# Decay and rate products of the RWKV-7 pairs issued in another order, and the key digits split later

## The reference, cut to what matters

```python
r = heads(xr @ w_rkv[0]); k = heads(xk @ w_rkv[1]); v = heads(xv @ w_rkv[2])
kk = l2_normalize(k * k_k)
for d in range(2):                       # the two directions
    logw = -softplus(-heads(w0[d] + tanh(xw @ w1[d]) @ w2[d])) - 0.5      # decay
    a = sigmoid(heads(a0[d] + (xa @ a1[d]) @ a2[d]))                      # rate
    kd = k * (1.0 + (a - 1.0) * k_a)
    dirs.append((exp(-exp(logw)), kd, -kk, kk * a))
# then, by direction: S <- S diag(w) + (S a) b^T + v k^T ; y = S r
```

## Time and profile before

| | |
|---|---|
| median of 3 runs | 2361.92 us |
| the profiled execution's own time | 2360.81 us |
| span of the profile | 2359.0 us |
| mean granted clock of PE | 0.991 |
| busy: PE, DVE, ACT, POOL | 97%, 66%, 54%, 9% |
| the RWKV-7 pairs | about 849 to 1320 us of the span |
| one pair | about 59 us |

### The profile page before, as it was taken

One profiled execution on the slowest core, in us unless ns is written; L12 is line 12 of the kernel. 1 busy time (PEld: TensorE's weight loads), 2 busy tenths in 40 slices (PEclk: granted clock), 3 DMA queues, 4 the chain that ended last, 5 costly groups with the idle time before them and its releaser, 6 DMA issues.

```text
span 2359.0 us, 57897 instructions
## 1 busy us (share of the span) xinstructions
PE 2285.1 (97%) x25130; PEld 1898.5 (80%) x25130; DVE 1561.0 (66%) x1768; ACT 1271.2 (54%) x1407; POOL 217.8 (9%) x208
## 2 busy tenths in 40 slices
PE   8999999999999889999998899999999999999998
PEld 5677566888888478888888788888888888888886
DVE  2544785322332766556666278888888888888888
ACT  4322024322222655555554277878777878777874
POOL 2000551000000041111112020000000000000010
PEclk9999999999999999999999999999999999999999
DMA  8466225333322521111102489999999999999994
GB/s 290 183 219 246 71 80 171 89 89 97 99 89 93 166 63 60 60 60 60 51 24 65 173 323 368 373 374 370 374 367 381 361 374 370 380 360 384 357 392 172
DMA packets 228493, 512.00 MB, mean 217 GB/s; under 512 B 15271, under 2 KB 108223, under 8 KB 228031
## 3 DMA queue, kind: packets, MB, share of 16 engines
q1 hardware_dynamic: 225470, 498.61, 58.3%
q10 hardware_dynamic: 1730, 7.10, 0.9%
q0 software_dynamic: 1152, 4.19, 0.6%
HBM read 492.58 MB, written 17.30 MB: 216 GB/s over the span
## 4 chain that ended last, share of the span: by engine, by line
PE 93%; DVE 3%; issue 1%; ACT 1%; DMA 1%; POOL 0%; ACTq 0%; DVEq 0%
PE bank L1700 27%; PE bank L1730 13%; PE bank L1205 3%; PE bank L1206 3%; PE bank L1207 3%; PE bank L1332 2%; PE bank L1111 2%; PE bank L1364 2%; PE bank L1082 2%; PE bank L1083 2%; PE bank L1084 2%; PE bank L1375 2%; PE bank L1223 2%; PE bank L1222 2%; PE bank L1224 2%
## 5 line engine op out<-in xcount | busy, mean ns | idle before, releaser
L3100 DVE TENSOR_TENSOR w_low<-expert_w,w_high 128x1792 fp32r<-128x1792 f32 (+2 forms) x384 | 771.8, 2024 | 121.4 <-ACT w_high L2250 118.5
L2250 ACT CAST w_high<-expert_w 128x1792 fp32r<-128x1792 f32 (+2 forms) x384 | 652.1, 1701 | 217.2 <-PE bank L1700 144.7
L1700 PE MATMUL bank<-w_high,xg_high 128*128 128x448 f32 x1024 | 294.3, 369 | 4.2 <-DVE xg_low L3090 4.2
L1700 PE MATMUL bank<-w_low,xg_high 128*128 128x448 f32 x1024 | 293.2, 368 | 0.0
L1700 PE MATMUL bank<-w_high,xg_low 128*128 128x448 f32 x1024 | 293.1, 367 | 0.0
L1700 PEld LDWEIGHTS bank<-w_high,xg_high 128*128 128x128 f32 x1024 | 191.6, 189 | 21.6 <-DVE xg_low L3090 4.4
L1700 PEld LDWEIGHTS bank<-w_high,xg_low 128*128 128x128 f32 x1024 | 192.8, 188 | 16.9
L1700 PEld LDWEIGHTS bank<-w_low,xg_high 128*128 128x128 f32 x1024 | 193.1, 189 | 15.8
L1730 PE MATMUL bank<-w_high,hid_high 128*128 128x512 f32 x448 | 175.8, 392 | 0.0
L1730 PE MATMUL bank<-w_high,hid_low 128*128 128x512 f32 x448 | 174.9, 390 | 0.0
L1730 PE MATMUL bank<-w_low,hid_high 128*128 128x512 f32 x448 | 174.7, 390 | 0.0
(11 more groups left out here) (440 smaller groups left out, 4109.3 us busy)
## 6 DMA issues: line engine op xcount, KB each, us to landing
expert_w<-in_moe_w_dram SPq DMA_DIRECT2D x128, 1792.0 KB, 9.6
expert_w<-in_moe_w_dram SPq DMA_DIRECT2D x32, 2048.0 KB, 10.3
arena<-in_mod_w_dram SPq DMA_DIRECT2D x48, 1024.0 KB, 8.6
expert_w<-in_moe_w_dram SPq DMA_DIRECT2D x32, 1536.0 KB, 10.0
arena<-in_ffn_w_dram SPq DMA_DIRECT2D x44, 512.0 KB, 5.1
slot_rows<-arena SPq DMA_DIRECT2D x25, 512.0 KB, 5.5
arena<-in_hy_w_in_dram SPq DMA_DIRECT2D x12, 1024.0 KB, 5.3
arena<-in_rw_w_rkv_dram SPq DMA_DIRECT2D x48, 256.0 KB, 2.8
```

The costliest lines, as they stand in the source:

```text
L1700: last = pe.matmul(bank[b0 + v][:, 0:EH], x[:, k, :], w_[:, kk, v * EH:v * EH + EH], start=(k == 0 and x is XGH and w_ is wh), stop=(k == ...
L2250: act.copy(high_piece(kind, n), piece(kind, ering[q % ERN], n // 2, n % 2))\
L3100: dve.tensor_tensor(piece(kind, low[s], n // 2, n % 2), piece(kind, ering[s], n // 2, n % 2), high_piece(kind, n).bitcast(F32), ALU.subtract)\
```

## The change

Four things are changed.

1. PE: `ahead_decay_and_rate` is replaced by `ahead_rate` and `ahead_decay`. The order is now decay 0, rate 0, rate 1, six fills, decay 1, each with its two column halves one behind the other. The rate of direction d goes to bank 6+d. The wait for `z_copy_0` is gone, and both rates wait for `z_copy_1`. The number of fills goes from 3 to 6, and two `settle` instructions go.
2. ACT takes the results in the order rate 0, rate 1, decay 0, decay 1.
3. POOL: the casts no longer stand before `ahead(0)` but behind the two small fills, directly before the subtractions.
4. PE: in pair 0 the wait tile by tile becomes one wait for all sixteen digit operations, ahead of the first keys product.

```diff
-PAIR_FILL, FIRST_FILL = 3, 4
+PAIR_FILL, FIRST_FILL = 6, 4
...
+            def in_halves(b, left, right):
+                for s in range(2):
+                    cs = slice(s * SEQ, s * SEQ + SEQ)
+                    last = mm(b[:, cs], left, right[:, cs], start=True, stop=True)
+                return last
             def ahead_keys(j):
+                if j == 1:
+                    pe.wait_ge(sem("digits_high"), 2 * KT)
                 step(pe, "ahead_vectors", "next_low", j - 1)
                 settle(pe)
                 for k in range(KT):
-                    if j == 1:
-                        pe.wait_ge(sem("digits_high"), KT + k + 1)
...
-            def ahead_decay_and_rate(j, d):
-                rate_bank = bank[6 + d]
...
-                step(pe, "pair_copies", f"z_copy_{d}", j - 1)
-                settle(pe)
-                for s in range(2):
-                    cs = slice(s * SEQ, s * SEQ + SEQ)
-                    decay = mm(bank[4 + d][:, cs], w2s[hd(d), :], HW[hd(d), cs], start=True, stop=True)
-                    rate = mm(rate_bank[:, cs], a2s[hd(1 - d), :], HA[hd(1 - d), cs], start=True, stop=True)
...
+            def ahead_decay(j, d):
                 if d == 0:
+                    step(pe, "ahead_copies", "key_copy", j)
+                else:
+                    step(pe, "pair_vectors", "bonus", j - 1)
+                in_halves(bank[4 + d], w2s[hd(d), :], HW[hd(d), :])\
+                    .then_inc(sem("ahead_products"), one("ahead_products", f"decay_{d}"))
+
+            def ahead_rate(j):
...
+                pe.wait_ge(sem("ld_pair"), j * LD_PAIR + LD_LORA)
+                ahead_decay(j, 0)
+                step(pe, "pair_copies", "z_copy_1", j - 1)
+                for d in range(2):
+                    in_halves(bank[6 + d], a2s[hd(d), :], HA[hd(d), :])\
+                        .then_inc(sem("ahead_products"), one("ahead_products", f"rate_{d}"))
+                if PAIR_FILL:
                     fill(PAIR_FILL)
...
                 if more:
-                    ahead_decay_and_rate(i + 1, 0)
-                    ahead_decay_and_rate(i + 1, 1)
+                    ahead_rate(i + 1)
+                    ahead_decay(i + 1, 1)
...
             def ahead_rates(j):                       # ACT
                 for d in range(2):
+                    step(act, "ahead_products", f"rate_{d}", j)
+                    act.activation(AS[d], bank[6 + d][:, :], ACT.Sigmoid, bias=dcol("rw_a0", j + 8 * d))\
+                        .then_inc(sem("ahead_copies"), one("ahead_copies", f"rate_sig_{d}"))
+                for d in range(2):
                     step(act, "ahead_products", f"decay_{d}", j)
...
             ahead_square(0)                           # POOL
-            step(pool, "ahead_products", "keys", 0)
-            pool.wait_ge(sem("ld_tail"), 16)
+            ahead(0)
             pool.wait_ge(sem("pair_done"), 1)
-            keys_high_digits()
-            ahead(0)
             pool.wait_ge(sem("lora_full"), 3)
             for h in range(2):
                 unit_blocks(h)
-            keys_low_digits()
+            step(pool, "ahead_products", "keys", 0)
+            pool.wait_ge(sem("ld_tail"), 16)
+            keys_digits()
```

More of the change, by code:

```diff
@@ L195, in _pair_steps @@
     pool = ["g_start_0", "g_start_1", "gate_copy", "eye_0", "eye_1"]
-    ahead_pe = ["keys", "decay_0", "rate_1", "decay_1", "rate_0", "key_sum", "values", "queries", "gate"]
-    ahead_act = ["key_copy", "decay_sig_0", "rate_sig_1", "decay_sig_1", "rate_sig_0", "key_log", "key_norm"]
+    ahead_pe = ["keys", "decay_0", "rate_0", "rate_1", "decay_1", "key_sum", "values", "queries", "gate"]
+    ahead_act = ["key_copy", "rate_sig_0", "rate_sig_1", "decay_sig_0", "decay_sig_1", "key_log", "key_norm"]
     ahead_act += ["e_incl_0", "e_inv_0", "e_excl_0", "e_incl_1", "e_inv_1", "e_excl_1"]
@@ L1293, in ahead_keys @@
                 last.then_inc(sem("ahead_products"), one("ahead_products", "keys"))
-            def ahead_decay_and_rate(j, d):
-                rate_bank = bank[6 + d]
-                if isinstance(j, int) and j == 0:
-                    pe.wait_ge(sem("gap_turned"), 2)
-                pe.wait_ge(sem("ld_pair"), j * LD_PAIR + LD_LORA)
+            def ahead_decay(j, d):
                 if d == 0:
@@ L1303, in ahead_decay_and_rate @@
                     step(pe, "pair_vectors", "bonus", j - 1)
-                step(pe, "pair_copies", f"z_copy_{d}", j - 1)
-                settle(pe)
-                for s in range(2):
-                    cs = slice(s * SEQ, s * SEQ + SEQ)
-                    decay = mm(bank[4 + d][:, cs], w2s[hd(d), :], HW[hd(d), cs], start=True, stop=True)
-                    rate = mm(rate_bank[:, cs], a2s[hd(1 - d), :], HA[hd(1 - d), cs], start=True, stop=True)
[L1310 to L1313, removed]
+                in_halves(bank[4 + d], w2s[hd(d), :], HW[hd(d), :])\
+                    .then_inc(sem("ahead_products"), one("ahead_products", f"decay_{d}"))
+            def ahead_rate(j):
+                if isinstance(j, int) and j == 0:
+                    pe.wait_ge(sem("gap_turned"), 2)
+                pe.wait_ge(sem("ld_pair"), j * LD_PAIR + LD_LORA)
[5 more added lines that the diff above has]
+                if PAIR_FILL:
                     fill(PAIR_FILL)
@@ L1326, in ahead_values @@
                     pe.wait_ge(sem("ld_pair"), j * LD_PAIR + LD_VALUES)
-                    step(pe, "ahead_copies", "rate_sig_1", j)
+                    step(pe, "ahead_copies", "rate_sig_0", j)
                     step(pe, "pair_vectors", "n_ready_1", j - 1)
@@ L1341, in ahead_queries @@
                     pe.wait_ge(sem("ld_pair"), j * LD_PAIR + LD_QUERIES)
-                    step(pe, "ahead_copies", "rate_sig_0", j)
+                    step(pe, "ahead_copies", "rate_sig_1", j)
                 for k in tiles:
@@ L1599, in _ @@
             pe.wait_ge(sem("lora_taken"), 2)
-            ahead_decay_and_rate(0, 0)
-            ahead_decay_and_rate(0, 1)
+            ahead_rate(0)
+            ahead_decay(0, 1)
             ahead_key_sum(0)
@@ L2071, in ahead_rates @@
                         .then_inc(sem("ahead_copies"), one("ahead_copies", f"decay_sig_{d}"))
-                    step(act, "ahead_products", f"rate_{1 - d}", j)
-                    act.activation(AS[1 - d], bank[6 + d][:, :], ACT.Sigmoid, bias=dcol("rw_a0", j + 8 * (1 - d)))\
-                        .then_inc(sem("ahead_copies"), one("ahead_copies", f"rate_sig_{1 - d}"))
             def ahead_key_log(j):
@@ L2351, in ahead, with keys_digits @@
                         .then_inc(sem("ahead_pool"), one("ahead_pool", f"b_raw_{d}"))
-            def keys_high_digits():
+            def keys_digits():
                 for k in range(KT):
                     pool.tensor_copy(keys_high[k], XK[:, k, :]).then_inc(sem("digits_high"), 1)
-            def keys_low_digits():
                 for k in range(KT):
```

## The result

The changed kernel takes 2377.69 us (median of 4 runs, 2375.84 to 2379.58), the kernel before in the same series 2361.36 us (4 runs): ratio 1.0068, 95% interval 1.0055 to 1.0082, some 16 us slower. The profiled execution took 2376.52 us itself, its span is 2374.7 us (before 2359.0). The forecast was 2380 us. Its sign and its two places were right. Both terms were too large, and something that was not in the sum filled part of the difference. One run of the experiments (late digits with waits by tile) took 3402.79 us at a granted clock of 0.615 and is left out of its ratio.

What follows compares the result with a forecast made beforehand. PE was taken to bound the kernel, busy 56.7 of 59.0 us a pair. Adding 8.1 us in pair 0 and 10.5 us in seven pair bodies, 18.6 us, to 2360.81 us gave about 2380 us, range 2373 to 2388.

Steps and rivals of the forecast that it cites:

- Both terms: Added time summed: 8.1 us in pair 0, and 10.5 us from seven pair bodies at 1.5 us each.
- Its sign: Whole kernel: the change makes it slower, given a chance of 0.93.
- its two places: PE's decay and rate products in the pairs, and PE's wait for POOL's digits in pair 0.
- The price of an unpaired pass: PE's decay and rate block: a pass without a partner costs a full step, 0.217 us.
- free passes: Decay and rate block: unpaired passes take half a step, so pairs add 0; 2370 us, chance 0.05.
- The number of steps: Decay and rate block: 15 steps in place of 8, so 1.5 us more in each pair.
- Fills at nothing: PE behind the decay and rate products: three added fills cost nothing.
- ACT's order, DVE's slack: In the pairs: decay 0 and DVE's scan come 1.8 us later, covered by 2.9 us available before n.
- Pair 0: PE waits for all 16 digit operations; keys product starts at 863.4, first level 870.9, 8.1 us later.
- not slower: Pair 0: digits are ready when PE comes and scores come earlier; total 2364 us, chance 0.04.
- The g gap: PE's idle time at the g product stays unchanged at 1.1 us a pair.
- The rival at 2373: At the g product the idle gap absorbs 1.1 of the 1.5 us per pair; chance 0.09.

Runs made afterwards that it cites:

- late digits with waits by tile: Kernel before with only POOL's casts moved behind b_raw and the fills, PE still waiting tile by tile: 2363.42 us, ratio 1.0005.
- The order alone: Changed kernel with POOL's order and PE's tile-by-tile waits of the kernel before, so only PE's and ACT's new order: 2373.96 us, ratio 1.0047.
- the two digit edits alone: Kernel before with POOL's casts behind b_raw and the fills and one PE wait for all sixteen digit operations: 2368.49 us, ratio 1.0025.
- The grouped order: Kernel before with both decay halves listed in a row, then both rate halves of the other direction, in each call: 2363.45 us, ratio 1.0001.
- the exchange of the two rates: Changed kernel with rate 1 listed ahead of rate 0 on PE and its sigmoid first on ACT: 2372.23 us, ratio 1.0045.

## Why the prediction was right, and where it was off

- **What bounds it.** Right. Time added on PE at the decay and rate block went through: +0.96 us in the block, +1.0 us a pair, and the 16.3 us at the end of the pairs still there at the first expert product. The order alone (11 us) and the two digit edits alone (5.9 us) add up to 17, near the 16.3 of all together.
- **The price of an unpaired pass.** Right: four further steps took 0.96 us, 0.24 each against the 0.217 forecast, so the partner was free. The rival "free passes" falls.
- **The number of steps: the step that failed.** I counted 15 steps because I let passes overlap only where they are neighbours in the list. The four passes of rate 0 and of rate 1 ran fully beside each other, so there are 12, and the term is 4 x 0.217 = 0.9 us a pair (measured 0.96) instead of 1.5; in seven bodies 6.7 instead of 10.5. The grouped order and the exchange of the two rates show the rule from both sides. The Trainium skill (TensorE: Matmul & The Clock Gate, Part 3: Packing small matmuls) says that matmuls start and end strictly in program order. The timeline with the grouped order shows the fifth in the list starting with the first; the starts there may be imprecise, but the time of the eight steps is not explained by that rule.
- **Fills at nothing.** Right for three. With 32 more it would have been badly wrong, though only part of the 73 us is at the fills themselves (30.1 us).
- **ACT's order, DVE's slack.** Right: the scan 1.8 us later, DVE idle 1.34 us ahead of n.
- **Pair 0.** Right in mechanism. Predicted were a last subtraction at 863.4, a keys product of 7.5 us and a first level at 870.9; measured 861.1, 8.5 and 869.7. The subtractions all ran at their shortest (9.81 for eight, not 10.5), the casts took 7.3 (not 7.7, nor the 8.8 worked out for full alternation with DVE), and b_raw ended earlier, since key_unit was done at 839.3 and not at 840.5. The slow start cost 1.9 us and not 0.9: from 861.2 to 867.0 the clock was 0.50. Counted from item 0 the delay is 7.6 us (6.87 + 0.77) against 8.1. By time, the two edits alone cost 5.9 us. The rival "not slower" falls here: the digits came 9.9 us after PE was ready for them.
- **The g gap.** It neither shrank nor gave way, as forecast (1.46 for 1.37 in pair 2, 8.9 for 7.6 us in seven). The rival at 2373 falls, and the run with 35 fills says why: the gap belongs to a count of instructions.
- **Not in the sum.** 0.8 us at L1381, and 1.08 us of gap plus 0.6 and 0.9 us at the lower clock around L1551 and L1415, less the 0.60 us gap that is gone: 2.8 us in this execution. In the span the terms are 7.6 + 6.7 + 2.8 = 17.1, less 0.8 from the early start and 0.6 that the span has made up behind the first expert product, which is the measured 15.7. That the forecast of 18.6 us comes this near is partly luck: the pairs' term was 3.8 us too large, and 2.8 us that nobody had counted made up for most of it. It is not shown that these 2.8 us come from the change. The grouped order, whose time is that of the kernel before, has longer gaps at the same two lines, and runs of the kernel before lie between 2357.6 and 2367.6 us in one series. What makes these gaps longer is open.

## What to carry to other kernels

When small products use half of PE's rows, look in the list at which half the next product uses: here a product ran free beside the one listed directly before it when that one sat in the other half, even with whole products one behind the other, and two neighbours of the same half did not overlap. A change from waits by tile to one wait cost a wait of 1.7 us while the producer was ahead and 9.9 us once it was late; read the producer's end against the consumer's start before merging waits. Put the price of a stall together with the clock behind it: after 9.9 us of idling PE ran its next 5.8 us at half clock.

## What the runs showed of the hardware that was not expected

- A product in the other 64 rows can start beside one listed four passes before it (1000.80 and 1000.81). It was not seen to start beside one further back: in the changed kernel rate 1 did not start beside decay 0, with rate 0 between them.
- An instruction that only increments a semaphore is not free in numbers: around the 35 in a row PE stood 3.8 us a time, 0.1 us each if the whole gap is theirs, while three or six vanish behind the passes in the array.
- PE's gaps without a releaser, 0.8 to 3.0 us, move with the count of its instructions (16 rows for 32 instructions). The Trainium skill (Runtime: NRT & Kernel Launch, Instruction fetch mechanics) says that instructions come in blocks of 256 and that the crossing is mostly hidden. The shift agrees with a fixed block, and so do the 127 rows between two gaps, each row a matrix instruction and a weight load: 254 instructions. In the kernels with three or six fills one such gap shows in each of the pairs 0 to 6, in 2024 rows. By the page's block that is an estimated sixteen crossings a pair (4047 / 256), so "mostly hidden" agrees in number; the one that shows takes 0.8 to 1.5 us. With 35 fills up to five show in a pair.
- Operations of POOL and of DVE, both with two inputs in SBUF, stretch each other: DVE 0.68 to 1.75 us, POOL's subtraction 1.25 alone and 2.24 at most. The Trainium skill (SBUF — State Buffer, Who interferes with whom) says that a DVE instruction with two SBUF inputs and a GpSimd instruction that reads SBUF exclude each other for a whole instruction; this agrees, as the added 1.07 us are nearly one subtraction.
